# Two decoder layers on one core: the LRU gate matmuls in four groups between the z projections instead of one block

## The chip, the cores and the metric

One core of one Trainium2 chip runs the whole program. The metric is the device time of one execution in microseconds; the median of three runs of a kernel is compared with the median of three runs of the other. Lower is better.

## The reference, cut to what matters

The reference computes one inference step of a two-layer decoder trunk for a prompt of 256 tokens and 8 single sample tokens, 264 columns in all. Each layer mixes with two recurrences side by side, a Mamba-2 SSD mixer and a Griffin RG-LRU mixer, and then applies a channel mixer: a dense SwiGLU in layer 0, and eight experts, two chosen per token, in layer 1. The part that the change touches is the gates of the LRU mixer:

```python
xb = xc.reshape(b, L, LRU_HEADS, LRU_BLOCK)
r = sigmoid(einsum('blhi,hij->blhj', xb, w_a).reshape(b, L, LRU_WIDTH) + b_a)
i = sigmoid(einsum('blhi,hij->blhj', xb, w_x).reshape(b, L, LRU_WIDTH) + b_x)
log_a = -LRU_C * r * softplus(-lam)
a = exp(log_a)
mult = sqrt(-expm1(2.0 * log_a))
u = mult * (i * xc)
...
_, h = associative_scan(combine, (a, u), axis=1)
```

Beside it stands the SSD mixer, which needs the projection `z`, a decay matrix per head (`exp` of differences of a cumulative sum), and for the sample tokens a state of 16 heads x 64 x 128 numbers each, which is read, decayed, updated and written back.

## The kernel before, in words

All activations stand transposed: 128 channels on the partitions and 264 tokens along the free axis, so that a width of 1024 is eight tiles, m = 0 to 7. Every engine has its own program in one fixed order, and semaphores join them. The accumulator memory (PSUM) has eight banks; `plan_fills` (L101) writes out by hand which bank each product fills and in which order, and counters `full` and `evac` for each bank carry the handover. A product may start in a bank only when the product before it in that bank has been read out.

Two banks, BA and BB, take all projections in turn, and the LRU gates too (the helper `tile`, L106). So every product in them waits until the product two before it has been read out.

The stretch around the change is the loop over the eight z tiles, once per layer (L962 on TensorE, L1287 on ScalarE, L1671 on VectorE):

- TensorE, for each m: the z projection of tile m into BA or BB (`project`, L813: eight weight tiles, each matmul recorded as two instructions); the matmuls "cum" that spread the cumulative sums of two heads over the partitions; for odd m a product `sam` (`spread_sample`, L848) that spreads the B and C rows of one sample token. After m = 2 (`LRU_GATES_AT`, L84) comes the block of gate matmuls, L972: for each of the eight tiles mt one matmul "ga" (for `r`) and one "gx" (for `i`), each 128x128 weights by 264 columns, 16 in a row into BA and BB in turn.
- ScalarE, for each m: it copies the z tile out of its bank; takes Exp of the two heads of tile m-1 (`seg`); for even m runs `start_sample` (L1223), a copy of the spread rows and eight scalings of a sample's state; at m = 2 reads out all 16 gate tiles with Sigmoid (L1295 to L1302); and from m = 3 on (`LRU_EXP_AT`, L85) takes Tanh and Exp of two tiles of `r` per m (L1305 to L1310).
- VectorE, for each m: it reads "cum" into `seg`, multiplies the previous `seg` tiles by the masked scores, at odd m updates a sample's state (`state`, L1561), and at m = 7 (`LRU_MULT_AT`, L86) computes the argument of the square root for all eight tiles, once the last Exp of `r` is done (`lru_exp`, L1690).
- POOL stores each new sample state, multiplies it out and loads the state of the sample after next; the loads are transfers queued behind that (L690).

After the loop TensorE projects the tiles of `gate`; after the second of them it computes the product "intra" and waits for the last `seg` tile of VectorE (`seg_done`, L990).

ScalarE evaluates Sigmoid, Exp, Tanh, Silu, Gelu and Sqrt from tables. Where the next function isn't in the loaded table set, the program holds an instruction ACT_TABLE_LOAD, placed by the compiler and not by the kernel's text.

Of the kernel before, what the change touches and what calls it, by code (L numbers as in the profile page):

```python
# [27 lines left out]
ACT = mybir.ActivationFunctionType  # L28
# [6 lines left out]
T = TP + NB  # L35
# [5 lines left out]
XT = 1024 // P  # L41
# [19 lines left out]
PA = dict(ln_mix=0, conv_w=8, conv_b=56, ssd_norm=68, lru_norm=76, ln_ffn=84, b_a=92, b_x=100, lam=108)  # L61
# [22 lines left out]
LRU_GATES_AT = 2  # L84
LRU_EXP_AT = 3  # L85
# [12 lines left out]
BY_VECTOR = (5, 7)  # L98


def plan_fills():  # L101

    pl = BankPlan()
    tiles = [0]

    def tile(*name):  # L106
        pl.add((BA, BB)[tiles[0] % 2], *name)
        tiles[0] += 1

    samples = [0] * LAYERS  # L110

    def sample(l):
        pl.add((BN, Q0)[samples[l] % 2], "sam", l, samples[l])
        samples[l] += 1

    for m in range(KD):
        tile("x", m)
    for i in range(4):
        pl.add(Q0 + i, "par", i)
    for l in range(LAYERS):  # L120
        pl.add(BN, "ln_mix", l)
        for m in range(XBC):
            tile("xbc", l, m)
        tile("dt", l)
        for m in range(XT):
            tile("xl", l, m)
            if m == SCAL_TILE:
                pl.add(Q0, "scal", l)
        for c in range(NC):
            for h in range(2):  # L130
                pl.add(Q1 + 2 * c + h, "xtok", l, c, h)
        pl.add(BN, "btok", l)
        pl.add(Q0, "cb", l)
        for c in range(NC):
            for g in range(GROUPS):
                pl.add(Q1 + 2 * c + g, "state", l, c, g)
        for i in range(5):
            pl.add((Q1, Q2, Q3, Q4, BN)[i], "rows", l, i)
        for i in range(2):
            pl.add((BN, Q0)[i], "final", l, i)  # L140
        sample(l)
        for g in range(GROUPS):
            tile("inter", l, g)
        for m in range(XT):
            tile("z", l, m)
            pl.add(Q1 + m % 4, "cum", l, m)
            if m in SAM_AT_Z:
                sample(l)
            if m == LRU_GATES_AT:
                for mt in range(XT):  # L150
                    tile("ga", l, mt)
                    tile("gx", l, mt)
        for m in range(XT):
            tile("gate", l, m)
            if m in SAM_AT_GATE:
                sample(l)
            if m == INTRA_AT:
                for c in range(NC):
                    for g in range(GROUPS):
                        pl.add(Q1 + 2 * c + g, "intra", l, c, g)  # L160
            if m == YT_AT:
                for i in range(4):
                    pl.add(Q1 + i, "yT", l, i)
            if m == HROWS_AT:
                for i in range(2):
                    pl.add(Q2 + i, "hrows", l, i)
        pl.add(Q1, "lru_norm", l)
        for g in range(GROUPS):
            pl.add((BN, Q0)[g], "ssd_norm", l, g)
        for m in range(KD):  # L170
            tile("out", l, m)
        pl.add(BN, "ln_ffn", l)
        if l == 0:
            for m in range(0, FT, 2):
                for kind in ("fg", "fu"):
                    for i in range(2):
                        tile(kind, m + i)
            for m in range(KD):
                tile("fd", m)
    pl.add(Q0, "logits")  # L180
    for t in range(3):
        for h in range(2):
            pl.add(Q1 + (2 * t + h) % 4, "hntok", t, h)
            pl.add((BA, BB)[(tiles[0] + h) % 2], "xtokf", t, h)
    pl.add(Q0, "rank")
    for i in range(2):
        pl.add(Q3 + i, "gather", i)
    return pl
# [61 lines left out]
def trunk(nc, a, o):  # L250

    with ExitStack() as ctx:
# [55 lines left out]
        gate_w = mixer_ctx.enter_context(nc.sbuf_tensor("gate_w", [P, 2, XT, P], F32))  # L308
# [24 lines left out]
        ig = carve(XT, T)  # L333
# [3 lines left out]
        xlc = carve(XT, T)  # L337
# [15 lines left out]
        rg = carve(XT, T)  # L353
# [171 lines left out]
        def col(l, table, name, i=0):  # L525
            base = 0 if table is PA else PA_ROWS
            c = base + table[name] + i
            return par[:, l, c:c + 1]
# [257 lines left out]
        def _(pe):  # L786
            def begin(*name):

                b, n = fill(*name)
                if n:  # L790
                    pe.wait_ge(evac[b], n)
                return bank[b]

            def done(ins, *name):
                ins.then_inc(full[fill(*name)[0]], 1)
# [5 lines left out]
            def mm(out, lhsT, rhs, start=True, stop=True):  # L801
                return nc.tensor.matmul(out, lhsT, rhs, start=start, stop=stop)  # L802
# [63 lines left out]
            for m in range(KD):  # L866
                out = begin("x", m)
# [6 lines left out]
            for g in range(4):  # L874
                out = begin("par", g)
# [5 lines left out]
            for l in range(LAYERS):  # L881
# [8 lines left out]
                out = begin("dt", l)  # L890
# [4 lines left out]
                for m in range(XT):  # L895
# [4 lines left out]
                    out = begin("scal", l)  # L900
# [13 lines left out]
                for c in range(NC):  # L914
                    for h in range(2):
                        out = begin("xtok", l, c, h)
# [3 lines left out]
                out = begin("btok", l)  # L920
                for c in range(NC):
                    for g in range(GROUPS):
                        i = 2 * c + g
# [3 lines left out]
                out = begin("cb", l)  # L927
                for c in range(NC):
                    for g in range(GROUPS):
                        i = 2 * c + g  # L930
# [31 lines left out]
                for m in range(XT):  # L962
                    project(("z", l, m), l, m, "z", lambda k: hn[:, k], KD)
                    out = begin("cum", l, m)
                    for i in range(2):
                        h = 2 * m + i
                        ins = mm(out[:, i * TP:(i + 1) * TP], ident[0:HEADS, h:h + 1].to_broadcast([HEADS, P]),
                                 dts[:, CUM, 0:TP])
                    done(ins, "cum", l, m)
                    if m in SAM_AT_Z:  # L970
                        spread_sample(l, SAM_AT_Z[m])
                    if m == LRU_GATES_AT:  # L972

                        pe.wait_ge(conv_ready, 22 * l + 22)
                        pe.wait_ge(gatew_landed, 64 * (l + 1))
                        for mt in range(XT):
                            for i, kind in enumerate(("ga", "gx")):
                                out = begin(kind, l, mt)
                                done(mm(out[:, 0:T], gate_w[:, i, mt, :], xlc[:, mt, :]), kind, l, mt)

                for m in range(XT):
                    project(("gate", l, m), l, m, "gate", lambda k: hn[:, k], KD)
# [214 lines left out]
        def _(act):  # L1197
            def filled(*name):
                b, n = fill(*name)
                act.wait_ge(full[b], n + 1)  # L1200
                return bank[b]

            def evacd(ins, *name):
                ins.then_inc(evac[fill(*name)[0]], 1)

            def evacuated(*name):
                b, n = fill(*name)
                act.wait_ge(evac[b], n + 1)

            def f(out, in_, fn=ACT.Copy, **kw):  # L1210
                return nc.scalar.activation(out, in_, fn, **kw)  # L1211
# [28 lines left out]
            for l in range(LAYERS):  # L1240
# [46 lines left out]
                for m in range(XT + 1):  # L1287
                    if m < XT:
                        evacd(f(ysz[:, m, :], filled("z", l, m)[:, 0:T]), "z", l, m)
                    if m > 0:  # L1290
                        evacuated("cum", l, m - 1)
                        f(seg[:, 2 * m - 2:2 * m], seg[:, 2 * m - 2:2 * m], ACT.Exp).then_inc(segexp_ready, 1)
                    if m in DECAY_AT_Z:
                        start_sample(l, DECAY_AT_Z[m])
                    if m == LRU_GATES_AT:  # L1295
                        act.wait_ge(rows_out, 64 * (l + 1))
                        act.wait_ge(final_out, 16 * (l + 1))
                        for mt in range(XT):
                            evacd(f(rg[:, mt, :], filled("ga", l, mt)[:, 0:T], ACT.Sigmoid, bias=col(l, PA, "b_a", mt)),
                                  "ga", l, mt)  # L1300
                            evacd(f(ig[:, mt, :], filled("gx", l, mt)[:, 0:T], ACT.Sigmoid, bias=col(l, PA, "b_x", mt)),
                                  "gx", l, mt)  # L1302
                        for i in range(2):
                            evacuated(("ga", "gx")[i], l, XT - 1)
                    if 0 <= m - LRU_EXP_AT < XT // 2:  # L1305
                        pair = (2 * (m - LRU_EXP_AT), 2 * (m - LRU_EXP_AT) + 1)
                        for mt in pair:
                            f(th[:, mt, :], rg[:, mt, :], ACT.Tanh, scale=ndecay8[:, l, mt:mt + 1])
                        for mt in pair:
                            f(rg[:, mt, :], rg[:, mt, :], ACT.Exp, scale=decay8[:, l, mt:mt + 1]).then_inc(lru_exp, 1)  # L1310
# [666 lines left out]
```

## Time and profile before

| | |
|---|---|
| median of three runs | 1937.28 us (1935.87, 1937.28, 1945.31) |
| span of the profiled execution | 1943.8 us |
| time of the profiled execution around its span | not given apart from the span; of the three runs only 1945.31 is longer than the span |
| TensorE busy | 1845.3 us, 95% of the span |
| VectorE busy | 1371.4 us, 71% |
| ScalarE busy | 1075.4 us, 55% |
| GpSimd busy | 167.2 us, 9% |
| mean granted TensorE clock | 0.963 |
| z loop of layer 0 | its three first tiles from 126.22 us of the span on, its end at 182.07 us |

The span is the time from the first to the last instruction of one execution. A time in the trace counts from the span's start. Layer 0 fills the span up to about 516 us, the mixer of layer 1 comes after it with the same order of work, and the experts of layer 1 take most of the rest.

### The profile page before, as it was taken

The page shows a single profiled execution, that of the slowest core. Times are in us where ns is not written, and L with a number is a line of the kernel's source. Part 1 is how long each engine was busy: PE and PEld are TensorE (multiplying, and loading weights), DVE is VectorE, ACT ScalarE, POOL GpSimd, SP SyncE. Part 2 cuts the span into 40 slices and gives each one's busy share as a digit, 9 for nine tenths or more (in the row PEclk, how much of TensorE's full clock was granted, in tenths as well). Part 3 has the DMA queues.
Part 4 walks back from the last instruction along what each step waited for, and adds up shares of the span by engine and source line. Part 5 has one row for each costly group of instructions (what it writes and reads, how often), then busy time and mean ns, then how long its engine had stood idle before and what let it go on. Part 6 is the DMA issues. An engine that isn't in the chain of part 4 may idle for free.

```text
span 1943.8 us, 24842 instructions
## 1 busy us (share of the span) xinstructions
PE 1845.3 (95%) x9284; PEld 1513.6 (78%) x9284; DVE 1371.4 (71%) x1458; ACT 1075.4 (55%) x1101; POOL 167.2 (9%) x175
## 2 busy tenths in 40 slices
PE   7989889999999988889999999999999999999996
PEld 5867778999886677868778778787787787787873
DVE  4655865554465487458879788788788787887883
ACT  2236444443222654346667577676676775776772
POOL 2014530000100453000000000000000000000000
PEclk9999889999999988879999999999999999999997
DMA  8424434555643443339979899799799798997980
GB/s 246 136 89 150 140 112 145 181 151 168 193 130 100 136 135 121 119 136 365 351 285 360 296 346 358 271 369 360 277 365 352 279 365 284 358 355 284 364 321 24
DMA packets 257030, 465.48 MB, mean 239 GB/s; under 512 B 8492, under 2 KB 108196, under 8 KB 256928
## 3 DMA queue, kind: packets, MB, share of 16 engines
q1 hardware_dynamic: 249384, 441.84, 65.6%
q0 software_dynamic: 6384, 21.28, 3.7%
q10 hardware_dynamic: 1192, 1.44, 0.3%
q8 instruction: 43, 0.70, 0.2%
q14 instruction: 27, 0.22, 0.0%
HBM read 453.70 MB, written 11.15 MB: 239 GB/s over the span
## 4 chain that ended last, share of the span: by engine, by line
PE 86%; DVE 8%; ACT 3%; issue 2%; ACTq 0%; DMA 0%; POOL 0%; DVEq 0%; POOLq 0%
PE bank L802 83%; DVE arena L1503 3%; PE bank L806 2%; DVE arena L1506 1%; ACT w_hi L1211 1%; ACT arena L1211 1%; DVE w_lo L1506 1%; DVE fw_lo L1506 1%; DMA arena<-in_state_lru_conv 0%; DVE rs L1506 0%; DVE rs L1760 0%; ACTq L592 0%; ACT L1211 0%; ACT moe_arena L1211 0%; DVE rs L1535 0%
## 5 line engine op out<-in xcount | busy, mean ns | idle before, releaser
L1506 DVE TENSOR_TENSOR w_lo<-wring,w_hi 128x2048 fp32r<-128x2048 f32 x336 | 768.3, 2290 | 128.9 <-ACT w_hi L1211 127.1
L1211 ACT ACTIVATE w_hi<-wring 128x2048 fp32r<-128x2048 f32 x336 | 643.7, 1919 | 248.7 <-PE bank L802 248.5
L802 PE MATMUL bank<-w_hi,xg_hi 128*128 128x512 f32 x896 | 370.9, 414 | 3.0 <-DVE xg_lo L1506 1.6
L802 PE MATMUL bank<-w_lo,xg_hi 128*128 128x512 f32 x896 | 351.0, 392 | 0.0
L802 PE MATMUL bank<-w_hi,xg_lo 128*128 128x512 f32 x896 | 349.9, 390 | 0.0
L802 PE MATMUL bank<-hn,wring 128*128 128x264 f32 x1152 | 273.1, 398 | 6.1 <-DVE hn L1503 6.1
L802 PEld LDWEIGHTS bank<-hn,wring 128*128 128x128 f32 x1152 | 223.1, 196 | 50.8 <-issue 9.8
L802 PEld LDWEIGHTS bank<-w_hi,xg_hi 128*128 128x128 f32 x896 | 168.9, 189 | 55.6 <-issue 16.5
L802 PEld LDWEIGHTS bank<-w_hi,xg_lo 128*128 128x128 f32 x896 | 169.3, 189 | 39.9 <-issue 7.7
L802 PEld LDWEIGHTS bank<-w_lo,xg_hi 128*128 128x128 f32 x896 | 168.7, 188 | 36.9
L1506 DVE TENSOR_TENSOR fw_lo<-wring,fw_hi 128x2048 fp32r<-128x2048 f32 (+1 forms) x54 | 115.2, 2134 | 109.7 <-ACT fw_hi L1211 109.7
L802 PE MATMUL bank<-w_hi,at_hi 128*128 128x512 f32 x448 | 175.1, 391 | 0.0
L802 PE MATMUL bank<-w_hi,at_lo 128*128 128x512 f32 x448 | 174.4, 389 | 0.0
L802 PE MATMUL bank<-w_lo,at_hi 128*128 128x512 f32 x448 | 174.3, 389 | 0.0
L1211 ACT ACTIVATE arena<-bank 128x264 f32<-128x264 f32 (+3 forms) x100 | 43.1, 444 | 218.5 <-PE bank L802 207.6
L802 PE MATMUL bank<-moe_arena 128*128 128x128 f32 (+2 forms) x540 | 142.4, 387 | 11.4 <-DVE moe_arena L1863 6.2
L1211 ACT ACTIVATE fw_hi<-wring 128x2048 fp32r<-128x2048 f32 (+1 forms) x54 | 94.8, 1756 | 89.8 <-PE bank L802 89.8
L802 PEld LDWEIGHTS bank<-moe_arena 128*128 128x128 f32 (+1 forms) x540 | 79.1, 194 | 45.2 <-issue 17.0
L802 PEld LDWEIGHTS bank<-w_lo,at_hi 128*128 128x128 f32 x448 | 84.1, 188 | 17.6
L802 PEld LDWEIGHTS bank<-w_hi,at_hi 128*128 128x128 f32 x448 | 84.1, 188 | 17.4
L802 PEld LDWEIGHTS bank<-w_hi,at_lo 128*128 128x128 f32 x448 | 84.1, 188 | 17.2
L773 POOL DMA_DIRECT2D out<-moe_arena x2 | 1.1, 534 | 1117.5 <-DVE moe_arena L1503 1117.5
(215 smaller groups left out, 2329.9 us busy)
## 6 DMA issues: line engine op xcount, KB each, us to landing
wring<-in_moe_w_gate SPq DMA_DIRECT2D x112, 1024.0 KB, 5.2
wring<-in_moe_w_up SPq DMA_DIRECT2D x112, 1024.0 KB, 5.3
wring<-in_moe_w_down SPq DMA_DIRECT2D x112, 1024.0 KB, 5.1
wring<-in_w_in SPq DMA_DIRECT2D x36, 1024.0 KB, 5.2
wring<-in_w_out SPq DMA_DIRECT2D x16, 1024.0 KB, 5.1
wring<-in_ffn_w_gate SPq DMA_DIRECT2D x11, 1024.0 KB, 5.3
wring<-in_ffn_w_up SPq DMA_DIRECT2D x11, 1024.0 KB, 5.4
wring<-in_ffn_w_down SPq DMA_DIRECT2D x16, 704.0 KB, 4.6
```

The lines of the kernel that those rows point to most:

```text
L773: pool.dma_start(o[0][0, t * P:(t + 1) * P, :], outt[:, t, :]).then_inc(y_out, 16)
L802: return nc.tensor.matmul(out, lhsT, rhs, start=start, stop=stop)
L806: return nc.tensor.transpose(out, in_, ident[0:k, 0:k])
L1211: return nc.scalar.activation(out, in_, fn, **kw)
L1503: return V.scalar_tensor_tensor(out=out, in0=in0, scalar=scalar, in1=in1, op0=op0, op1=op1)
L1506: return V.tensor_tensor(out, in0, in1, op)
```

## The change

The function `gate_pair(m)` names the two tiles whose gates belong behind z tile m: tiles 0 and 1 at m = 2, 2 and 3 at m = 3, 4 and 5 at m = 4, 6 and 7 at m = 5, none otherwise. The bank plan, TensorE and ScalarE all follow it: behind z tiles 2 to 5 (the third to the sixth) stand four gate matmuls and four Sigmoids each. Tanh and Exp stay where they were, one z tile behind their gates. The number of matmuls, of activations and of DMAs written in the kernel is unchanged, and so is the alternation of BA and BB.

```diff
+def gate_pair(m):
+    p = 2 * (m - LRU_GATES_AT)
+    return (p, p + 1) if 0 <= p < XT else ()
...
 # plan_fills
-            if m == LRU_GATES_AT:
-                for mt in range(XT):
-                    tile("ga", l, mt)
-                    tile("gx", l, mt)
+            for mt in gate_pair(m):
+                tile("ga", l, mt)
+                tile("gx", l, mt)
...
 # TensorE
                     if m == LRU_GATES_AT:
                         pe.wait_ge(conv_ready, 22 * l + 22)
                         pe.wait_ge(gatew_landed, 64 * (l + 1))
-                        for mt in range(XT):
-                            for i, kind in enumerate(("ga", "gx")):
-                                out = begin(kind, l, mt)
-                                done(mm(out[:, 0:T], gate_w[:, i, mt, :], xlc[:, mt, :]), kind, l, mt)
+                    for mt in gate_pair(m):
+                        for i, kind in enumerate(("ga", "gx")):
+                            out = begin(kind, l, mt)
+                            done(mm(out[:, 0:T], gate_w[:, i, mt, :], xlc[:, mt, :]), kind, l, mt)
...
 # ScalarE
                     if m == LRU_GATES_AT:
                         act.wait_ge(rows_out, 64 * (l + 1))
                         act.wait_ge(final_out, 16 * (l + 1))
-                        for mt in range(XT):
-                            evacd(f(rg[:, mt, :], filled("ga", l, mt)[:, 0:T], ACT.Sigmoid, bias=col(l, PA, "b_a", mt)),
-                                  "ga", l, mt)
-                            evacd(f(ig[:, mt, :], filled("gx", l, mt)[:, 0:T], ACT.Sigmoid, bias=col(l, PA, "b_x", mt)),
-                                  "gx", l, mt)
-                        for i in range(2):
-                            evacuated(("ga", "gx")[i], l, XT - 1)
+                    for mt in gate_pair(m):
+                        evacd(f(rg[:, mt, :], filled("ga", l, mt)[:, 0:T], ACT.Sigmoid, bias=col(l, PA, "b_a", mt)),
+                              "ga", l, mt)
+                        evacd(f(ig[:, mt, :], filled("gx", l, mt)[:, 0:T], ACT.Sigmoid, bias=col(l, PA, "b_x", mt)),
+                              "gx", l, mt)
                     if 0 <= m - LRU_EXP_AT < XT // 2:
-                        pair = (2 * (m - LRU_EXP_AT), 2 * (m - LRU_EXP_AT) + 1)
+                        pair = gate_pair(m - LRU_EXP_AT + LRU_GATES_AT)
+                        evacuated("ga", l, pair[1])
+                        evacuated("gx", l, pair[1])
```

## Rows read from the trace of the kernel before

**Rows 1.** The page, parts 1 and 4: busy time by engine, chain by engine.
```profile
PE 1845.3 (95%) x9284; PEld 1513.6 (78%) x9284; DVE 1371.4 (71%) x1458; ACT 1075.4 (55%) x1101; POOL 167.2 (9%) x175
...
PE 86%; DVE 8%; ACT 3%; issue 2%; ACTq 0%; DMA 0%; POOL 0%; DVEq 0%; POOLq 0%
```

**Rows 2.** The chain that ended last, in order of time, 123 to 197.
```profile
146.16 35.99 PE bank L802 x144
...
182.18 1.13 DVE arena L1677 x4
...
195.44 0.61 DVE arena L1506
```

**Rows 3.** Stretches of the z loop: busy time by engine, clock, DMA share.
```profile
141.55:156.22 14.67, 11.21 (x33) 5.82 (x33) 2.26 (x5) 11.16 (x25) 5.82 (x6) 0.88 0.26 72
156.22:182.07 25.85, 25.85 (x118) 19.88 (x117) 12.60 (x36) 17.93 (x46) 13.32 (x12) 1.00 0.47 143
...
633.13:647.80 14.67, 11.15 (x33) 5.83 (x33) 2.27 (x5) 11.16 (x25) 5.84 (x6) 0.88 0.25 71
```

**Rows 4.** TensorE in order of time: start, us, line, operation, [idle before, releaser].
```profile
141.55 1.16 PE L802 MATMUL bank<-arena,gate_w 128*128 128x264 f32 x4
146.16 10.08 PE L802 MATMUL bank<-arena,gate_w 128*128 128x264 f32 x28 [3.46 <-ACT arena L1211]
...
148.09 1.51 PE L802 MATMUL bank<-arena,gate_w 128*128 128x264 f32 x3
...
156.22 3.83 PE L802 MATMUL bank<-hn,wring 128*128 128x264 f32 x16
159.98 1.12 PE L802 MATMUL bank<-dts,ident 16*128 16x256 f32 x4
161.03 1.16 PE L802 MATMUL bank<-ident,arena 128*128 128x128 f32 x8
162.03 3.73 PE L802 MATMUL bank<-hn,wring 128*128 128x264 f32 x16
```

**Rows 5.** ScalarE in order of time, 140 to 164.
```profile
141.88 2.44 ACT L1211 ACTIVATE arena<-arena,hexp 128x128 f32<-128x128 f32 x8
144.34 1.28 ACT L1211 ACT_TABLE_LOAD   x1
...
147.45 0.48 ACT L1211 ACTIVATE arena<-bank,par 128x264 f32<-128x264 f32 x1 [0.96 <-PE bank L802]
...
150.55 1.07 ACT L1211 ACTIVATE arena<-bank,par 128x264 f32<-128x264 f32 x2 [0.21 <-PE bank L802]
...
160.17 0.39 ACT L1211 ACTIVATE arena<-bank 128x264 f32<-128x264 f32 x1 [3.41 <-PE bank L802]
160.57 1.28 ACT L1211 ACT_TABLE_LOAD   x1
161.87 0.63 ACT L1211 ACTIVATE arena<-arena 128x512 f32<-128x512 f32 x1
162.41 0.91 ACT L1211 ACTIVATE arena<-arena,ndecay 128x264 f32<-128x264 f32 x2
```

**Rows 6.** ScalarE in order of time, around the gate projections.
```profile
200.29 1.28 ACT L1211 ACT_TABLE_LOAD   x1
211.98 0.39 ACT L1211 ACTIVATE arena<-bank 128x264 f32<-128x264 f32 x1 [10.41 <-PE bank L802]
```

**Rows 7.** Short stretches around the stalls, columns as in rows 3.
```profile
118.00:122.00 4.00, 2.56 (x21) 1.56 (x20) 2.12 (x4) 2.61 (x5) 0.00 (x0) 1.00 0.00 0
142.00:146.00 4.00, 0.70 (x4) 0.26 (x2) 1.92 (x5) 3.97 (x10) 3.76 (x4) 1.00 0.33 97
146.00:149.00 3.00, 2.83 (x6) 1.81 (x7) 0.00 (x0) 1.45 (x4) 1.61 (x3) 0.50 0.13 19
149.00:150.00 1.00, 1.00 (x4) 0.56 (x4) 0.00 (x0) 0.62 (x2) 0.00 (x0) 0.80 0.80 201
```

**Rows 8.** ScalarE behind the z loop, waiting for a state load.
```profile
188.32 2.45 ACT L1211 ACTIVATE arena<-arena,hexp 128x128 f32<-128x128 f32 x8 [3.87 <-DMA arena<-in_state_ssd]
```

## The prediction, made blind

> **What bounds the kernel now.** I read the page first. TensorE is busy for 95% of the span and holds 86% of the chain that ended last [rows 1], so a microsecond of TensorE's idle time inside a layer is normally a microsecond of the kernel. Then the chain in order of time: it runs on TensorE from 146.16 to the end of the z loop, goes over to VectorE at 182.18 and stays there until 196.05, where the last multiplication of a `seg` tile lets TensorE go on [rows 2]. VectorE takes over exactly when TensorE delivers the last "cum", so whatever the z loop gains or loses moves the whole rest of the layer. Then the stretches: the block of 16 gate tiles takes 14.67 us in each layer, the remaining five z tiles 25.85 us at full clock with TensorE busy throughout [rows 3].
>
> How long would 16 gate tiles last if nothing held them? A z projection gives it: its 16 instructions of the same shape take 159.98 - 156.22 = 3.76 us [rows 4], so a gate tile (two instructions) is 0.47 us and the block 7.5 us. The block thus holds 14.67 - 7.5 = 7.1 us of waiting per layer. It has two causes. First, ScalarE reaches the first Sigmoid late: the eight scalings of the sample's state and a table load stand before it, and TensorE idles 3.46 us, until 146.16 [rows 4, 5]. Second, the two banks: in the steady part ScalarE starts a pair of Sigmoids every 1.07 + 0.21 = 1.28 us [rows 5], since each tile waits for the one two before it; of that 0.48 is one Sigmoid and 0.80 is the matmul with both handovers. That is 0.64 us per tile against 0.47.
>
> **The change, part by part.** It adds and removes no matmul, no activation, no byte of DMA. It moves 12 of the 16 matmuls and Sigmoids per layer, and adds table loads.
>
> *Table loads.* Exp to Sigmoid costs a load (144.34), Sigmoid to Exp another (160.57, and the next activation starts at 161.87, 1.30 us later) [rows 5]; Tanh behind Exp costs none. Before, that is two per layer. After, every z tile from 2 to 5 goes Exp, then Sigmoid, then Tanh or Exp: one load at m = 2, three at m = 3 (for `seg`, for Sigmoid, for Tanh), two each at m = 4 and 5. Eight instead of two, 6 x 1.3 = 7.8 us of ScalarE per layer. Whether they count depends on their place, so I replay layer 0 by its rows. A load doesn't wait for the matmul whose result needs it: the one at 200.29 ran at once, though its Gelu had to wait 10.41 us for TensorE [rows 6].
>
> *Group at m = 2.* Nothing changes up to its third tile, so TensorE starts that at 146.16. z tile 3 can start where tile ga2 started, 148.09 [rows 4], since the Sigmoid of ga1 ends at 147.93 [rows 5]. 148.09 - 141.55 = 6.54 us. The granted clock is 0.50 from 146 to 149 and 0.80 on the mean of 149 to 150, after the stretch in which TensorE was busy 0.70 of 4 us [rows 7]: it is at 1.2 instead of 2.4 GHz until about 149.4. Before, the slow stretch hid behind ScalarE's rhythm; now z tile 3 stands in it for 1.3 us and loses half, 0.6 us. Sum 7.14. z ends at 148.09 + 3.76 + 0.6 = 152.45; "cum" adds 161.03 - 159.98 = 1.05 and the sample product 162.03 - 161.03 = 1.00 [rows 4]: the next group starts at 154.50.
>
> *Group at m = 3.* ScalarE copies z 0.19 us after its end (160.17 against 159.98), goes on after 0.40, loads the table (1.30), takes Exp (162.41 - 161.87 = 0.54), loads again (1.29), and ends its first Sigmoid 0.48 later [rows 4, 5]: 152.45 + 4.20 = 156.65. The next Sigmoid of the same bank ends 1.28 later, 157.93, and z tile 4 starts at 157.98. The group takes 3.48 us.
>
> *Group at m = 4.* It starts at 157.98 + 3.76 + 1.05 = 162.79. ScalarE has copied, taken Exp, and again has a sample to scale before the load and the Sigmoids: the very sequence of m = 2 (Tanh and Exp of the pair before end by 161.5, ahead of the z tile). So it costs what that did: 6.54 and, if the clock falls after an idle time of the same 3.6 us, 0.6 more, 7.14. I take it. z tile 5 ends at 173.69, the group at m = 5 starts at 175.74.
>
> *Group at m = 5.* No sample here. ScalarE is through copy, Exp and load at 173.69 + 0.19 + 0.40 + 0.54 + 1.29 = 176.11; the matmul's result (175.74 + 0.80) comes later. The two rounds then end at 177.02 and 178.30: 2.61 us.
>
> *Sum.* 7.14 + 3.48 + 7.14 + 2.61 = 20.37 us instead of 14.67: 5.7 us more per layer. Layer 1 has the same 14.67 [rows 3] and the same order, so 11.4 us in all.
>
> *The terms that cost nothing.* VectorE sat waiting for TensorE in the loop (12.60 us busy of 25.85 [rows 3]); `seg` and states of z tiles 3 and 4 merely come earlier. Its step at m = 7 needs the last Exp of `r`: ScalarE ends that near 187.5 in the replay, VectorE asks at about 191.8; if m = 6 took ScalarE 4 us longer, it would count one for one. POOL's stores and state loads follow the VectorE updates; the moved matmuls issue no DMA, and SyncE's weight loads wait for z tiles, of which 3 and 4 come earlier and 5 to 7 later, with six slots ahead. The extra `evacuated` waits are for Sigmoids of an earlier z tile, long ended.
>
> *Bounds.* Not shown: the clock in the new gaps. If it doesn't fall at m = 4, z tile 5 keeps its 0.6 and the round there takes 0.5 less: 4.6 per layer, 9.2 in all. If it also falls in the gaps at m = 3 and 5, each costs one slower round (0.5) and half of some 3.3 us (1.6): 4.2 more per layer, 9.9, or 19.8 in all. The nearest rows speak against that: TensorE busy 2.56 of 4.00 us left the clock at 1.00 [rows 7], and these groups are busy 1.9 of 3.5 us and more.
>
> The durations are from an execution with a span of 1943.8 us; its time around the span isn't shown, and the median is 6.5 below that span. 0.3% of 11 us is nothing, so the sum goes on the median as it is: 1937.28 + 11.4 = 1948.7.
>
> A rule stands against the change: the Trainium skill, "ScalarE: Activation LUTs", section "Rules for kernel authors", says to group activations by table set and finish one set before switching. Here eight switches stand in place of two, and by the replay three of them stand between TensorE and a bank that it waits for, at m = 3 and 4. The same page ("What ACT_TABLE_LOAD costs") prices a switch at about 2.66 us with a drain; this trace shows 1.30 from load to next start, and the sum uses that.
>
> **The rivals.**
>
> *The gates hide behind the z projections (faster).* This would be so if ScalarE reached each Sigmoid as the matmul ended and the z tiles covered the bank handovers. The place is the bank wait of the third gate tile and of the next z tile in each group. At best all 7.1 us of waiting per layer go: 1937.28 - 14.3 = 1923.0. The point that decides is 14.67 / 4 = 3.67 us per group: below it the change wins. For it: the stretch has TensorE busy only 11.21 of 14.67 us. Against it: the 2.44 us of scalings stand before the Sigmoids at m = 2 and 4. Even with the added loads at no price the sum is 7.14 + 2.6 + 5.9 + 2.6 = 18.2, above 14.67. Chance 0.04.
>
> *Part of the loss is given back later (no change).* ScalarE waits 3.87 us for a state load behind the loop [rows 8]. The state update that frees the load is at m = 5, and a gate group now stands between it and that wait, which shrinks by 2.6 us. If the rest of the layer followed ScalarE, 5.2 us would come back: 1943.5. Against it: the chain there is VectorE's, without a gap [rows 2]. Chance 0.20.
>
> *The clock falls in every group (slower still).* Worked out above: 1957.1. Chance 0.10.
>
> *A switch is dearer in this place.* Were each load twice its row, the two at m = 3, the one at m = 4 and 0.9 of the one at m = 5 would add 1.3 each, 5.1 per layer, 10.2 in all: 1958.9. No gap behind a load is in the rows. The 2.66 us that the Trainium skill states ("ScalarE: Activation LUTs", "What ACT_TABLE_LOAD costs") would give about this; the trace doesn't agree. Chance 0.02.
>
> *The change does nothing:* only if the compiler found one set with Sigmoid and Exp, which the two loads of rows 5 exclude; even then the banks hold. Inside the second rival.
>
> **How the numbers follow.** A measurement of this kernel can tell about 0.5% (9.7 us) from no change, so slower begins at 1947.0 and faster below 1927.6. The forecast has the remaining 0.64, by itself from 1944.5 to 1953.5: its low end is the 9.2 us case with the median's own scatter, its high end adds a low clock in one group per layer. About 0.53 of that 0.64 lies above 1947.0. With the third and fourth rival slower has 0.65, no change 0.31, faster 0.04. The range takes in the second rival and most of the third: 1941.5 to 1956.5.
>
> **What would show it.** Right: eight table loads per z loop; TensorE idle near 3.5 us before the third gate tile at m = 2 and again at m = 4, released by ScalarE; half clock behind the first; "cum" of tile 7 some 5.7 us later after the group's start, and the stretch from there to "intra" unchanged near 14 us. Wrong: a z loop of unchanged or shorter length, a group at m = 4 without the gap, or a stretch behind the loop that differs by more than 2 us.

## The result, and the profile of the changed kernel

| | before | after |
|---|---|---|
| median | 1938.57 us (6 runs, 1935.87 to 1946.82) | 1956.94 us (6 runs, 1952.06 to 1957.83) |
| ratio | | 1.0085, 95% interval 1.0067 to 1.0103 |
| profiled execution | span 1943.8 | 1956.1 us, span 1954.1 |
| z loop, first gate matmul to end of the last "cum", layer 0 / layer 1 | 40.52 / 40.52 | 47.63 / 47.82 |
| ACT_TABLE_LOAD from m = 2 to 6, each layer | 2 | 8 |

The kernel became slower, by 0.85%: 16.5 us on 1938.57, with an interval from 13.0 to 20.0. The ratio is not the quotient of the two medians, which lie 18.4 us apart. The median itself, 1956.94, stands just above the range that was forecast (its upper end is 1956.5); the ratio on the median that the prediction started from gives 1953.7, inside it.

The page of the kernel after, parts 1 and 4. ScalarE has 12 instructions and 16 us more; TensorE is as busy as before, with idle time between. ScalarE's share of the chain rose from 3% [rows 1] to 5%.

```profile
PE 1845.8 (94%) x9284; PEld 1519.3 (78%) x9284; DVE 1368.9 (70%) x1458; ACT 1091.1 (56%) x1113; POOL 167.6 (9%) x175
...
PE 85%; DVE 7%; ACT 5%; issue 2%; DMA 1%; ACTq 0%; POOL 0%; DVEq 0%; POOLq 0%
```

The stretches of the z loop of the kernel after, with the columns of [rows 3]: length, busy time of TensorE's matmuls, of its weight loads, of VectorE, ScalarE and POOL, then the granted clock of TensorE (1.00 is the 2.4 GHz level, 0.50 the 1.2 GHz level, values between are means over both), the DMA share and GB/s. The clock of the whole loop fell to 0.89 on the mean; in the kernel before it was 0.88 in the block and 1.00 behind it, 0.96 together. The stretch behind the loop, up to "intra", is 14.10 us against 14.12 before (182.07 to 196.19): the chain goes over to VectorE at the last "cum" and hands all of the delay on.

```profile
143.21:190.84 47.63, 39.16 (x150) 28.11 (x149) 13.55 (x41) 36.90 (x77) 20.53 (x20) 0.89 0.34 101
190.84:204.94 14.10, 10.90 (x65) 9.75 (x65) 13.82 (x21) 11.13 (x18) 9.16 (x7) 0.99 0.71 219
...
144.00:147.80 3.80, 0.37 (x2) 0.00 (x0) 1.58 (x3) 3.77 (x10) 3.56 (x4) 0.86 0.26 77
147.80:149.75 1.95, 1.92 (x5) 1.28 (x5) 0.00 (x0) 0.83 (x2) 1.48 (x3) 0.50 0.00 0
149.75:155.33 5.58, 5.58 (x17) 4.22 (x16) 0.00 (x0) 0.48 (x1) 0.00 (x0) 0.66 0.34 97
```

TensorE of the kernel after in order of time, as in [rows 4]. The two rows with 3.46 us of idle time are the third gate tile at m = 2 and at m = 4. Behind them the z projections (x16) take 155.33 - 149.75 = 5.58 and 176.70 - 171.97 = 4.73 us instead of 3.76.

```profile
143.21 1.16 PE L807 MATMUL bank<-arena,gate_w 128*128 128x264 f32 x4
147.83 2.13 PE L807 MATMUL bank<-arena,gate_w 128*128 128x264 f32 x4 [3.46 <-ACT arena L1215]
149.75 5.66 PE L807 MATMUL bank<-hn,wring 128*128 128x264 f32 x16
155.33 1.12 PE L807 MATMUL bank<-dts,ident 16*128 16x256 f32 x4
156.39 1.16 PE L807 MATMUL bank<-ident,arena 128*128 128x128 f32 x8
157.38 1.06 PE L807 MATMUL bank<-arena,gate_w 128*128 128x264 f32 x4
159.62 1.16 PE L807 MATMUL bank<-arena,gate_w 128*128 128x264 f32 x4 [1.18 <-ACT arena L1215]
160.90 3.83 PE L807 MATMUL bank<-hn,wring 128*128 128x264 f32 x16
164.66 1.12 PE L807 MATMUL bank<-dts,ident 16*128 16x256 f32 x4
165.72 1.16 PE L807 MATMUL bank<-arena,gate_w 128*128 128x264 f32 x4
170.33 1.85 PE L807 MATMUL bank<-arena,gate_w 128*128 128x264 f32 x4 [3.46 <-ACT arena L1215]
171.97 4.79 PE L807 MATMUL bank<-hn,wring 128*128 128x264 f32 x16
176.70 1.12 PE L807 MATMUL bank<-dts,ident 16*128 16x256 f32 x4
177.75 1.16 PE L807 MATMUL bank<-ident,arena 128*128 128x128 f32 x8
178.75 2.34 PE L807 MATMUL bank<-arena,gate_w 128*128 128x264 f32 x8
181.21 3.83 PE L807 MATMUL bank<-hn,wring 128*128 128x264 f32 x16
```

ScalarE of the kernel after at m = 3. Three loads stand in one turn: for Exp, for Sigmoid, and for Exp again. The last stands behind Tanh (the rows with ndecay), not ahead of it as the prediction had it.

```profile
155.44 0.39 ACT L1215 ACTIVATE arena<-bank 128x264 f32<-128x264 f32 x1 [4.96 <-PE bank L807]
155.85 1.28 ACT L1215 ACT_TABLE_LOAD   x1
157.14 0.63 ACT L1215 ACTIVATE arena<-arena 128x512 f32<-128x512 f32 x1
157.79 1.28 ACT L1215 ACT_TABLE_LOAD   x1
159.09 0.85 ACT L1215 ACTIVATE arena<-bank,par 128x264 f32<-128x264 f32 x2
160.37 0.93 ACT L1215 ACTIVATE arena<-bank,par 128x264 f32<-128x264 f32 x2 [0.43 <-PE bank L807]
161.19 0.91 ACT L1215 ACTIVATE arena<-arena,ndecay 128x264 f32<-128x264 f32 x2
162.11 1.28 ACT L1215 ACT_TABLE_LOAD   x1
```

### The profile page after: what moved, and what is told of

The parts are those of the page before. It is cut to its first block, busy times and chain, and to the rows that moved or that the text cites. A ratio compares the mean times of both kernels' runs of the same rounds, so it can differ in the third digit from the quotient of the medians.

```text
span 1954.1 us, 24860 instructions
## 1 busy us (share of the span) xinstructions
PE 1845.8 (94%) x9284; PEld 1519.3 (78%) x9284; DVE 1368.9 (70%) x1458; ACT 1091.1 (56%) x1113; POOL 167.6 (9%) x175
## 4 chain that ended last, share of the span: by engine, by line
PE 85%; DVE 7%; ACT 5%; issue 2%; DMA 1%; ACTq 0%; POOL 0%; DVEq 0%; POOLq 0%
PE bank L807 82%; DVE arena L1507 3%; PE bank L811 2%; ACT arena L1215 2%; ACT w_hi L1215 1%; DVE w_lo L1510 1%; DVE arena L1510 1%; ACT L1215 1%; DVE fw_lo L1510 1%; DMA arena<-in_state_lru_conv 1%; DVE rs L1510 0%; DVE rs L1764 0%; ACTq L597 0%; ACT moe_arena L1215 0%; DVE rs L1539 0%
## 5 line engine op out<-in xcount | busy, mean ns | idle before, releaser
L807 PE MATMUL bank<-hn,wring 128*128 128x264 f32 x1152 | 279.7, 404 | 6.6 <-DVE hn L1507 6.1
L807 PEld LDWEIGHTS bank<-hn,wring 128*128 128x128 f32 x1152 | 227.7, 200 | 55.2 <-issue 9.1
L807 PE MATMUL bank<-moe_arena 128*128 128x128 f32 (+2 forms) x540 | 137.9, 378 | 11.4 <-DVE moe_arena L1867 6.2
```

## The experiments

All compare one stretch, from the first gate matmul to the end of the last "cum", in both layers. In this section m and "group" are as in the change. The ratio is that to the kernel before, as run beside the version in question: e1 to e4 stand against 33 runs of it with a median of 1938.37 us, e5 to e7 against 23 others with 1939.02.

| | edit | stretch, layer 0 / 1 | median, us | ratio to before, 95% |
|---|---|---|---|---|
| before | | 40.52 / 40.52 | 1938.57 | |
| after | | 47.63 / 47.82 | 1956.94 | 1.0085 (1.0067 to 1.0103) |
| e1 | after, idle time filled | 43.84 / 43.85 | 1948.23 | 1.0044 (1.0025 to 1.0064) |
| e2 | after, sample behind the gates | 42.38 / 42.62 | 1945.45 | 1.0032 (1.0018 to 1.0047) |
| e3 | after, no table switch | 42.77 / 43.85 | 1942.63 | 1.0018 (1.0002 to 1.0035) |
| e4 | after, both | 36.20 / 36.20 | 1935.40 | 0.9974 (0.9958 to 0.9990) |
| e5 | before, sample behind the block | 37.47 / 37.48 | 1934.76 | 0.9972 (0.9954 to 0.9989) |
| e6 | before, both | 36.20 / 36.20 | 1934.79 | 0.9962 (0.9945 to 0.9979) |
| e7 | e4, groups over four banks | 32.97 / 32.97 | 1929.25 | 0.9944 (0.9927 to 0.9962) |

**e1: fill the idle time.** Seven matmuls whose result is overwritten stand in the gap, in a bank of "cum" that is free.

```diff
                     for mt in gate_pair(m):
+                        if m in (2, 4) and mt % 2:
+                            free = begin("cum", l, m + 1)
+                            for _ in range(7):
+                                mm(free[:, 0:T], gate_w[:, 0, mt, :], xlc[:, mt, :])
```

> The kernel after with seven further matmuls of 128x264 (their result is overwritten, nothing reads it) between the second and the third gate tile at m = 2 and m = 4, where TensorE otherwise idles 3.46 us; at 0.47 us each they last 3.3 us, so they fit in. I read the stretch from the first gate matmul to the end of the last cum of the z loop: 40.5 us before, 47.6 after. Theory A (the idle time lowers the granted clock, and the low clock makes the z tiles behind it slow): the clock stays at 1.00, z tile 3 takes 3.8 us instead of 5.6, z tile 5 3.8 instead of 4.7, the third and fourth gate tiles come a little sooner: about 44.5 us, and about 6 us off the time of the kernel after. Theory B (the slow z tiles have another cause, such as a transfer or the banks): 47.6 us or more.

Measured: 43.84 us with TensorE doing more work, and 1948.2 us as the median, 8.7 below the kernel after. The stretch as a whole, and z tile 3 in it (columns as above):

```profile
140.10:183.94 43.84, 41.34 (x177) 30.51 (x176) 13.57 (x41) 36.82 (x77) 20.56 (x20) 1.00 0.37 110
...
146.00:149.76 3.76, 3.76 (x16) 2.96 (x16) 0.00 (x0) 0.40 (x1) 0.57 (x1) 1.00 0.45 139
```

The clock stays at 1.00 and z tile 3 takes 3.76 instead of 5.58 us. Nothing else was changed for that tile: its banks, its weights and ScalarE's order are the same. The slow z tiles come from the idle time ahead of them, through the granted clock. The low clock costs the kernel after 3.8 to 4.0 us a layer; in layer 0 2.8 of them are in z tiles 3 and 5 and 1.0 in the third and fourth gate tiles. Theory B falls. These 3.8 us are not all new: the block of the kernel before pays 1.1 us to the low clock too (e5). So an estimate for layer 0 is that of the 7.1 us that the loop lost 2.7 are added low clock and 4.4 added waiting. The gain was larger than expected, 3.8 us of the stretch against 3.1 and 8.7 of the median against 6.

**e2: the sample's work behind the Sigmoids.**

```diff
-                    if m in DECAY_AT_Z:
-                        start_sample(l, DECAY_AT_Z[m])
...
                         evacd(f(ig[:, mt, :], filled("gx", l, mt)[:, 0:T], ACT.Sigmoid, bias=col(l, PA, "b_x", mt)),
                               "gx", l, mt)
+                    if m in DECAY_AT_Z:
+                        start_sample(l, DECAY_AT_Z[m])
```

> The kernel after with start_sample moved behind the Sigmoids of the same m on ScalarE; same instructions, same eight table loads per layer. Theory A (the copy and eight scalings of a sample stand ahead of the Sigmoids at m = 2 and 4, 3.0 us of the idle time each, and bring the low clock): groups of about 3.0, 3.5, 3.0 us, and up to 6.3 at m = 5, where ScalarE now comes late with its backlog; the stretch is 41 to 42 us, the time about 12 us below the kernel after, near that of before. Theory C (the six added table loads are what costs): no load is gone, so the stretch stays above 46 us.

Measured: 42.38 and 42.62, with all eight loads still there. TensorE of e2, the third gate tiles at m = 2, 3, 4 and 5:

```profile
143.64 1.16 PE L807 MATMUL bank<-arena,gate_w 128*128 128x264 f32 x4 [1.49 <-ACT arena L1215]
...
152.97 1.16 PE L807 MATMUL bank<-arena,gate_w 128*128 128x264 f32 x4 [1.18 <-ACT arena L1215]
...
160.87 1.16 PE L807 MATMUL bank<-arena,gate_w 128*128 128x264 f32 x4 [0.65 <-ACT arena L1215]
...
171.02 1.35 PE L807 MATMUL bank<-arena,gate_w 128*128 128x264 f32 x4 [1.60 <-ACT arena L1215]
```

The 3.46 us are gone, the rest of the waiting is there, and at m = 5 a wait of 1.60 appears: ScalarE arrives late from the scalings, Tanh, Exp and a load. That group took 4.35 us, where up to 6.3 had been expected; the one at m = 2 took 3.93 instead of 3.0, since its table load started only when the first gate matmul had ended. Behind the wait of 1.60 z tile 6 took 5.20 us in layer 0 and 3.76 in layer 1. Order alone gives back 5.2 us a layer, so theory C alone doesn't hold; but theory A's 41 to 42 us were missed by 0.4 to 0.6. The median is 11.5 us below the kernel after, as expected.

**e3: no table switch.** Both gates by (1 + tanh(x/2)) / 2. The halves go into the scales and biases of the steps behind them, so nothing is left out.

```diff
-    f(rg[:, mt, :], filled("ga", l, mt)[:, 0:T], ACT.Sigmoid, bias=col(l, PA, "b_a", mt))
+    f(rg[:, mt, :], filled("ga", l, mt)[:, 0:T], ACT.Tanh, scale=0.5, bias=col(l, PA, "b_a", mt))
...
-    f(th[:, mt, :], rg[:, mt, :], ACT.Tanh, scale=ndecay8[:, l, mt:mt + 1])
+    f(th[:, mt, :], rg[:, mt, :], ACT.Tanh, scale=ndecay8[:, l, mt:mt + 1], bias=ndecay8[:, l, mt:mt + 1])
...
-    f(th[:, :, :], th[:, :, :], ACT.Sqrt)
+    f(th[:, :, :], th[:, :, :], ACT.Sqrt, scale=0.25)
...
-    link(tt(ig[:, :, :], ig[:, :, :], xlc[:, :, :], ALU.mult))
+    link(stt(ig[:, :, :], ig[:, :, :], 1.0, xlc[:, :, :], ALU.add, ALU.mult))
```

(Gx, Exp, `decay8`, `ndecay8` and the two bias tables are treated alike; the 1.0 written into `th` becomes 0.5.)

> The kernel after with both gates by the identity sigmoid(x) = (1 + tanh(x/2)) / 2, its halves folded into the biases, the scales and the square root, so that the z loop needs one table set: the same number of activations, no table load between z tiles 2 and 6. Theory A: each group loses only the loads that stand before its Sigmoids, 1.3 us at m = 2 and 4 and 0.9 at m = 3, and some of the low clock: 43 to 44.5 us for the stretch, still 2.5 us or more above the 40.5 of before; time 6 to 9 us below the kernel after. Theory C (the table loads carry the loss): the stretch is at or below 40.5 us.

Measured: 42.77 and 43.85, above the 40.52 of before in both layers. The two layers differ by 1.1 us with the same instructions, through the clock (columns as above):

```profile
139.62:182.39 42.77, 38.07 (x149) 27.19 (x148) 13.54 (x41) 27.09 (x68) 20.37 (x20) 0.92 0.37 112
633.37:677.22 43.85, 39.28 (x150) 28.02 (x149) 13.56 (x41) 27.13 (x68) 20.43 (x20) 0.88 0.36 108
144.73:149.00 4.27, 4.27 (x17) 3.33 (x17) 0.00 (x0) 0.48 (x1) 1.04 (x2) 0.86 0.43 123
162.81:168.25 5.44, 5.44 (x16) 4.05 (x16) 0.00 (x0) 2.37 (x5) 0.00 (x0) 0.69 0.35 96
```

The idle time at m = 2 and 4 is now 2.03 us, and the clock still falls behind it: the last two rows are z tiles 3 and 5, with 4.27 and 5.44 us instead of 3.76. So the loads alone aren't the loss either; without any of them the loop is longer than with the block. Layer 0 lies a little below the 43 to 44.5 us that were expected. The time was misjudged: the median is 14.3 us below the kernel after, where 6 to 9 had been expected, and the two loops give only 8.8 of it.

**e4: both edits.**

> Both edits together in the kernel after: no table load in the loop and start_sample behind the gates. Theory A: groups of about 2.6, 2.6, 2.6 and 3.8 us, no low clock, a stretch of 37.5 us, 3 us per layer below the kernel before, and a time some 6 us below it (0.3%). Theory D (the bank handover alone, two banks for six products in a row, makes groups dearer than the block however early ScalarE comes): the stretch stays at 40.5 us or above.

Measured: 36.20 us in both layers at full clock, 11.5 below the kernel after and 4.3 below the one before. The four groups took 2.65, 2.47, 2.57 and 2.46 us; the last was expected at 3.8, and the stretch with it at 37.5. TensorE's idle time in the loop is 36.20 - 35.11 = 1.1 us. Layer 0 (layer 1 has the same length and clock):

```profile
141.20:177.40 36.20, 35.11 (x149) 25.05 (x149) 13.66 (x41) 27.30 (x68) 20.37 (x20) 1.00 0.45 133
```

Theory D falls: the groups can be cheaper than 14.67 us with two banks. The two edits give more together (11.5) than one by one (5.2 and 4.4 on the mean): each alone leaves idle time that lowers the clock. The kernel as a whole gains 0.26%, 5 us (3.0 between the medians), of the 8.6 us that both loops gained. Outside the two loops its profile has 1863.4 us and the first profile of before 1862.8, and between these two the gain arrives: the spans are 1935.8 and 1943.8, 8.0 us apart. Other executions of the kernel before are shorter outside the loops (e0).

**e5 and e6: the same edits on the block.** e5 moves `start_sample` behind the block, e6 has the tanh gates as well. They ask what the grouping itself is worth.

> The kernel before (one block of 16 gate tiles) with start_sample of m = 2 moved behind the block on ScalarE. Theory A (the sample's scalings ahead of the first Sigmoid make TensorE's idle time and the low clock): the third gate tile starts 2.6 us after the first instead of 4.6, as in e2, and the other rounds keep 1.28 us a pair at full clock, so the block takes 11.6 us instead of 14.67 and the stretch 37.5 instead of 40.5; 6 us off the time. If the order of the sample were no matter for the block, 40.5.

> The kernel before with both edits: gates by tanh (no table load around the block) and start_sample behind the block. It tells what the grouping itself is worth, since e4 is the same with four groups. Theory A: the block takes 1.4 + 7 rounds of 1.28 = 10.4 us against the 10.2 of e4's four groups, a stretch of 36.4 us against e4's 36.2; the time of e4 within 0.1%. Theory E (the groups spread ScalarE's work and that is where e4's gain comes from): the stretch stays 2 us or more above e4's 36.2.

Measured: 37.47 for e5 and 36.20 for e6, the same 36.20 as e4; the medians of e6 and e4 differ by 0.03%. TensorE of e5 from the third gate tile on, behind 1.49 us of idle time:

```profile
142.82 8.86 PE L802 MATMUL bank<-arena,gate_w 128*128 128x264 f32 x28 [1.49 <-ACT arena L1211]
151.81 3.83 PE L802 MATMUL bank<-hn,wring 128*128 128x264 f32 x16
```

These 14 tiles take 151.81 - 142.82 = 8.99 us at full clock. In the kernel before the same 14 took 156.22 - 146.16 = 10.06 [rows 4], behind 3.46 us and partly at half clock. So the low clock cost the block 1.07 us. TensorE of e6 has the whole block in two rows:

```profile
140.51 1.16 PE L802 MATMUL bank<-arena,gate_w 128*128 128x264 f32 x4
141.88 8.86 PE L802 MATMUL bank<-arena,gate_w 128*128 128x264 f32 x28 [0.21 <-ACT arena L1211]
150.87 3.83 PE L802 MATMUL bank<-hn,wring 128*128 128x264 f32 x16
```

The block takes 150.87 - 140.51 = 10.36 us. The four groups of e4 take 10.15 together, but two of the z tiles behind them take 3.76 us instead of 3.66 and use that up, and the whole stretch is equal to a hundredth of a microsecond. So once ScalarE comes in time, spreading the gates over two banks is worth nothing by itself, and theory E falls. And e5 shows that moving one call in the kernel before, with no change to the arithmetic, gains 3 us a layer.

**e7: groups over four banks.** The third and fourth tile of a group go to banks of "cum", which are free then.

```diff
             for mt in gate_pair(m):
-                tile("ga", l, mt)
-                tile("gx", l, mt)
+                if mt % 2:
+                    pl.add(Q1 + (m + 1) % 4, "ga", l, mt)
+                    pl.add(Q1 + (m + 2) % 4, "gx", l, mt)
+                else:
+                    tile("ga", l, mt)
+                    tile("gx", l, mt)
```

> e4 with the third and fourth tile of each group in two of the four banks of cum, so that no gate tile waits for a Sigmoid of its own group. Theory A (what is left in e4 is the two-bank handover): a group takes 4 x 0.47 = 1.9 us instead of about 2.5, a stretch of 33.5 us instead of 36.2, 5.4 us less in all and a time near 1930. Rival: ScalarE or the sample chain becomes the limit and the stretch stays at 36, or the stretch shrinks and VectorE hands the gain back behind the loop.

Measured: 32.97 us, no idle time of TensorE left in the stretch, and a median of 1929.25 us, the lowest here; the ratio puts it 0.56% below the kernel before.

```profile
140.70:173.67 32.97, 32.97 (x149) 25.96 (x148) 14.06 (x41) 27.14 (x68) 20.09 (x20) 1.00 0.48 144
```

A group is 142.59 - 140.70 = 1.89 us of TensorE at m = 2:

```profile
140.70 2.05 PE L811 MATMUL bank<-arena,gate_w 128*128 128x264 f32 x8
142.59 3.72 PE L811 MATMUL bank<-hn,wring 128*128 128x264 f32 x16
```

Both halves of the rival fall: the stretch shrank, and the one behind the loop, up to "intra", is 187.77 - 173.67 = 14.10 us as before. A block over the same additional banks was not run, so e7 shows what the banks are worth to the groups, and not that groups are needed to use them.

**e0: the kernel before once more, for a second profile.**

> The kernel before, unchanged, for a second profile: its runs so far lie near 1936 or near 1945. If the two levels come from the low clock at the end of the program, a profile of the lower level has the same z loops (40.5 us each) and a last stretch, from the end of layer 1's mixer on, some 5 us or more shorter than 1143.6.

Measured: 1935.88 us, span 1933.9, 9.9 below the first profile of the same kernel. The expectation was right on the last stretch and wrong on the loops, which took 41.10 and 41.09 us. First the two rows of the first profile of before, then two of e0: the projections ahead of layer 0's loop, and everything behind layer 1's mixer.

```profile
28.62:141.55 112.93, 108.21 (x521) 85.01 (x521) 66.77 (x166) 31.09 (x72) 4.49 (x7) 0.98 0.43 134
800.20:1943.80 1143.60, 1113.65 (x4960) 878.85 (x4958) 914.00 (x678) 746.34 (x516) 2.19 (x4) 0.97 0.85 304
```

```profile
28.97:140.30 111.33, 107.43 (x521) 84.83 (x521) 66.74 (x166) 30.93 (x72) 4.51 (x7) 0.98 0.43 134
795.30:1933.90 1138.60, 1108.61 (x4960) 877.79 (x4958) 913.80 (x678) 746.29 (x516) 2.20 (x4) 0.98 0.85 306
```

The last stretch is 5.0 us shorter, the one ahead of layer 0's loop 1.6 and that ahead of layer 1's 2.9 (114.16 and 111.25 us), while the loops are 0.6 longer each. All that lies outside the two loops takes 1862.8 us in the first profile and 1851.7 in the second, 11.1 us less with the same instructions. In the last stretch the whole difference is TensorE's busy time, 1108.61 us instead of 1113.65. Part of it can be seen at the very end: in the last 24 us the clock was 0.52 in the first profile and 0.82 in e0, where 23 matmuls ran in the time of 11 (the first profile, then e0):

```profile
1920.00:1943.80 23.80, 10.15 (x11) 1.69 (x10) 8.15 (x12) 5.61 (x10) 1.58 (x3) 0.52 0.12 46
1910.00:1933.90 23.90, 8.92 (x23) 3.02 (x21) 8.15 (x12) 6.70 (x12) 1.58 (x3) 0.82 0.13 48
```

In the loop the block took 155.60 - 140.26 = 15.34 us, against 14.67 in the first profile, with the same idle time in front (TensorE of e0 in order of time):

```profile
140.26 1.16 PE L802 MATMUL bank<-arena,gate_w 128*128 128x264 f32 x4
144.88 10.88 PE L802 MATMUL bank<-arena,gate_w 128*128 128x264 f32 x28 [3.46 <-ACT arena L1211]
155.60 3.75 PE L802 MATMUL bank<-hn,wring 128*128 128x264 f32 x16
```

The same instructions take other times, by which of them meet the low clock.

## Why the prediction was right, and where it was off

- **Direction and mechanism** were right: slower, by ScalarE reaching the Sigmoids late and TensorE waiting in front of them, twice per layer, with the delay handed on whole by VectorE.
- **Size:** 11.4 us were forecast; the two loops lost 7.1 + 7.3 = 14.4, and the runs show 16.5 with an interval from 13.0. The forecast lies below that interval.
- **Group at m = 2:** 149.75 - 143.21 = 6.54 us, as worked out. **At m = 3:** 160.90 - 157.38 = 3.52 against 3.48. **At m = 5:** 181.21 - 178.75 = 2.46 against 2.61. **At m = 4:** 171.97 - 165.72 = 6.25 against 6.54: its third and fourth tile met the low clock only in part (0.82 on the mean of 170 to 171 us).
- **The term that was mis-sized** is the low clock behind the idle time. The prediction read from the block of before how long the clock stayed low (until 149.4 [rows 7]), placed 1.3 us of that in z tile 3 and took 0.6 us. Measured is 5.58 - 3.76 = 1.82 us in layer 0 and 2.02 in layer 1 for z tile 3, and 0.97 and 1.15 for z tile 5. e1 takes the idle time away and with it all of both. e0 shows why one profile misled: in another execution of the kernel before the clock stayed low for longer behind the same 3.46 us, until about 150.5, that is 5.6 us from the third gate tile on instead of 3.2, and the block took 0.67 us more. In the kernel after it was 5.8 us at m = 2 and 3.7 at m = 4. In layer 0 the sum closes with that: 5.7 us forecast, 1.6 more in z tiles 3 and 5, 0.4 less in the groups and 0.2 more since z tiles 4 and 6, now behind a group, take 3.76 and not 3.66 make the measured 7.1.
- **The waiting in the block** was read with two causes, and it had three. 3.46 us of idle time and 14 tiles at 0.64 instead of 0.47 us come to 5.8, not 7.1. Most of the rest is the low clock, which the prediction said had hidden behind ScalarE's rhythm; by e5 it cost the block 1.07 us.
- **Table loads:** eight instead of two, as forecast, 1.28 us each in the row and 1.29 to 1.30 from a load to the next start (157.79 to 159.09); no gap behind one, so the rival of the dearer switch is out. A load was taken to run ahead of the wait for the matmul. So it did at m = 5 (load at 177.73, its Sigmoid at 179.39, released by TensorE), but in e2 the one at m = 2 started only when the matmul had ended (141.81 us, 0.85 idle, released by TensorE); in the kernel after, the sample's work covers that.
- **What costs nothing:** VectorE, POOL and SyncE were judged rightly; the last Exp of `r` ended at 190.42, 4.3 us before VectorE's step on it at 194.68, as forecast (187.5 and 191.8), and the stretch behind the loop kept its 14.1 us. The second rival (a give-back through the state load) had its step right, since that wait of ScalarE shrank from 3.87 us [rows 8] to 0.60, and its effect was nil.
- **The third rival** (a low clock in every group) is out too: z tiles 4 and 6, behind the groups at m = 3 and 5, took 164.66 - 160.90 and 184.97 - 181.21, 3.76 us both.
- **The rule of the Trainium skill** ("ScalarE: Activation LUTs", "Rules for kernel authors", finish one table set before switching) points the right way here: e3, without the switches, has a stretch 4.4 us shorter on the mean, of the 7.2 lost. But it doesn't tell the whole, since e3's stretch is still longer than that with the block. The price on the same page of the Trainium skill ("What ACT_TABLE_LOAD costs"), 2.66 us a switch with a drain, is not what these rows show: 1.29.
- **The faster rival** gave 3.67 us per group as the point that decides. e4's groups are below it (2.54 on the mean) and e4 is faster than before. But the point leaves out the z tiles behind the groups: the groups of e3 take 5.11, 2.46, 4.48 and 2.47 us in layer 0, 3.63 on the mean, and still its stretch is 2.25 us longer than before, by z tiles 3 and 5, which the low clock made slow.

What stays open: the difference between the 14.4 us of the loops and the 16.5 of the runs. It lies inside the interval, and e0 shows that executions of one kernel differ by more than that outside the loops, 11.1 us. The profile of the kernel after has 1858.7 us there, between the 1862.8 and the 1851.7 of the two profiles of before; no run separates the change from this scatter. It also stays open what sets how long the clock stays low: the runs show 3.2 to 5.8 us behind the same 3.46 us of idle time.

## What to carry to other kernels

Before spreading matmuls between other work, look at who reads them out and what that engine does just before. Here the reader had a table switch ahead of every group and a sample's scaling ahead of two, and these two paid the 3.46 us that one block paid once. Price an idle time of TensorE with the slow stretch behind it, and note that products that bounce between two banks cost the same in a block as in groups (e4 and e6). More banks made the groups faster (e7); whether a block would gain as much from them was not tried.

## What the runs showed of the hardware

- Idle time of TensorE can cost twice. Behind 3.46 us of waiting the granted clock was 0.50, the 1.2 GHz level, and a projection of 16 matmuls took 5.58 us instead of 3.76; with the wait filled by useless matmuls it took 3.76 (e1). Behind 2.03 us it fell too (e3, z tiles of 4.27 and 5.44 us). The length of the gap alone doesn't decide: behind 1.49 us in e2 z tile 3 took 148.68 - 144.93 = 3.75 us in layer 0 and 644.69 - 639.25 = 5.44 in layer 1, and behind 1.49 us in e5 the block ran at full clock in both.
- The Trainium skill ("TensorE: Matmul & The Clock Gate", Part 1) says that the number of slow matmuls at the start of a kernel changes from run to run. These traces show the like behind an idle time in its middle: the block of the kernel before took 14.67 us in one execution and 15.34 in another.
- The times of the same kernel fall into two clusters: of 33 runs of the kernel before 24 took 1935 to 1942 us and nine 1945 to 1948. A profile of each shows that parts outside the loops take 111.3 or 112.9 us and 1138.6 or 1143.6 us; in the last 24 us the granted clock was 0.82 or 0.52. Changes of 0.3% should be read from stretches, not from a single time.
- Tanh ran from the table set of Sigmoid (in the kernel after the load stands behind Tanh, at 162.11) as well as from that of Exp (no load between Exp at 161.87 and Tanh at 162.41 [rows 5]).
